# Ten f32 products per half on TensorE in the first block's attention, with a result that nobody reads

## The reference

```python
def mixer_ab(h, w_in, ...):        # layer 0
    qa, ka, va, qb, kb, vb = jnp.split(h @ w_in, AB_SPLITS, axis=-1)
    oa = causal_block_attention(qa, ka, va, map_w, bias_a)   # 4 heads, two softmax maps each
    oa = oa * lax.rsqrt(jnp.mean(jnp.square(oa), -1, keepdims=True) + LN_EPS)
    ob = dilated_attention(qb, kb, vb, table)                # 8 heads of 64
    return jnp.concatenate([oa, ob], axis=-1) @ w_o

def mixer_cd(h, w_in, ...):        # layer 1
    oc = moba_attention(qc, kc, vc, table)                   # 8 heads of 64, causal with 256 tokens
    od = causal_block_attention(qd, kd, vd, ones, fox_bias)  # 8 heads, forget bias
    return jnp.concatenate([oc, od], axis=-1) @ w_o
```

## Time and profile before

| | |
|---|---|
| median of 3 runs | 2954.01 us |
| profiled execution, its own time | 2952.88 us |
| its span, first to last instruction | 2950.4 us |
| mean granted TensorE clock | 0.932 of full |
| attention of layer 0, first score to last values | 160.8 to 222.1 us |
| attention of layer 1, first score to last values | 595.9 to 672.1 us |
| f32 products as records | two records each on TensorE; a transpose leaves one |

### The profile page before, as it was taken

The page is one execution under the profiler, slowest core; times in us unless marked ns, Lnnn a source line. Parts: engine busy times, 40 slices in busy tenths (PEclk is TensorE's granted clock), DMA queues, the critical chain, the costliest instruction groups (busy, mean ns, idle before and its releaser), DMA issues. The chain is left out here.

```text
span 2950.4 us, 39864 instructions
## 1 busy us (share of the span) xinstructions
PE 2676.7 (91%) x15451; PEld 2244.4 (76%) x15451; DVE 1807.7 (61%) x3288; ACT 1078.8 (37%) x2037; POOL 225.2 (8%) x167
## 2 busy tenths in 40 slices
PE   4757998998999799998998889999899998998899
PEld 4736997867998588886855668887688886856899
DVE  6567776537776656545748476554566544847554
ACT  2343543433443323223226343322333222326553
POOL 2000100000100201001000020000110000100110
PEclk8868998957999899999989999999999999889999
DMA  8923874802675144332720133433343433720453
GB/s 290 281 75 128 269 254 128 266 29 101 234 243 194 50 150 143 125 121 83 212 72 1 44 100 129 157 122 107 100 143 129 153 111 107 208 77 19 144 178 132
DMA packets 355605, 413.92 MB, mean 140 GB/s; under 512 B 25708, under 2 KB 292629, under 8 KB 355353
## 3 DMA queue, kind: packets, MB, share of 16 engines
q1 hardware_dynamic: 353326, 404.37, 42.6%
q0 software_dynamic: 736, 4.58, 0.5%
q10 hardware_dynamic: 1354, 2.43, 0.2%
HBM read 409.75 MB, written 5.27 MB: 141 GB/s over the span
## 5 line engine op out<-in xcount | busy, mean ns | idle before, releaser
L636 DVE TENSOR_TENSOR weight_lo<-raw_weights,weight_hi 128x512 fp32r<-128x512 f32 x1024 | 776.6, 765 | 902.9 <-ACT weight_hi L1164 892.5
L1164 ACT ACTIVATE weight_hi<-raw_weights 128x512 fp32r<-128x512 f32 x1024 | 633.0, 629 | 1336.9 <-PE bank L841 1186.4
L841 PE MATMUL bank<-H_hi,weight_hi 128*128 128x256 f32 (+1 forms) x2832 | 970.3, 343 | 116.1 <-POOL H_lo L802 82.6
L841 PE MATMUL bank<-H_lo,weight_hi 128*128 128x256 f32 (+1 forms) x2832 | 952.4, 336 | 0.0
L841 PE MATMUL bank<-H_hi,weight_lo 128*128 128x256 f32 (+1 forms) x2832 | 952.3, 336 | 0.0
L841 PEld LDWEIGHTS bank<-H_hi,weight_hi 128*128 128x128 f32 x2832 | 553.8, 196 | 193.5 <-issue 115.2
L841 PEld LDWEIGHTS bank<-H_hi,weight_lo 128*128 128x128 f32 x2832 | 554.3, 196 | 51.0
L841 PEld LDWEIGHTS bank<-H_lo,weight_hi 128*128 128x128 f32 x2832 | 555.3, 196 | 48.5 <-issue 0.5
L1451 DVE SCALAR_TENSOR_TENSOR ada_partial<-raw_weights,silu_c,ada_partial 128x512 f32<-128x512 f32 x672 | 477.8, 742 | 1.2 <-DVE ada_partial L1451 0.2
L841 PE MATMUL bank<-hidden_hi,weight_hi 128*128 128x256 f32 (+1 forms) x1056 | 361.2, 342 | 3.4 <-DVE weight_lo L636 3.4
L841 PE MATMUL bank<-hidden_hi,weight_lo 128*128 128x256 f32 (+1 forms) x1056 | 357.7, 339 | 0.0
(11 more groups left out here) (165 smaller groups left out, 2103.1 us busy)
## 6 DMA issues: line engine op xcount, KB each, us to landing
raw_weights<-in_w_ada_dram SPq DMA_DIRECT2D x120, 1024.0 KB, 5.4
raw_weights<-in_w_ffn_up_dram SPq DMA_DIRECT2D x88, 1024.0 KB, 5.3
raw_weights<-in_w_ffn_in_dram SPq DMA_DIRECT2D x44, 1024.0 KB, 5.7
raw_weights<-in_w_ffn_down_dram SPq DMA_DIRECT2D x32, 1024.0 KB, 5.1
raw_weights<-in_w_in_dram SPq DMA_DIRECT2D x18, 1024.0 KB, 7.9
raw_weights<-in_w_ffn_out_dram SPq DMA_DIRECT2D x16, 1024.0 KB, 7.7
raw_weights<-in_w_in_ab_dram SPq DMA_DIRECT2D x12, 1024.0 KB, 9.1
raw_weights<-in_w_in_cd_dram SPq DMA_DIRECT2D x12, 1024.0 KB, 7.6
```

Source lines behind the costliest of these rows:

```text
L636: eng.tensor_tensor(WL[:, p.g % SPLIT, 0:p.kt * CW].rearrange("p (t n) -> p t n", n=CW), raw_ap(ch.n, ch.kt, CW)[:, p.k0:p.k0 + p.kt, :], ...
L841: return pe.matmul(o, w, x, start=start, stop=stop, skip_group_check=True)
L1164: act.activation(WH[:, p.g % SPLIT, 0:p.kt * CW].rearrange("p (t n) -> p t n", n=CW), raw_ap(ch.n, ch.kt, CW)[:, p.k0:p.k0 + p.kt, :], ACT ...
```

## The change

`attn` gets a helper `busy(h, n)` that issues n products of `ident` with `ones`, 128x128 by 128x128 in f32, into the bank that the next `turn` overwrites. It signals nothing and nothing reads its result. It acts where a half has fewer than four key blocks and `vrow` is D, that is in layers 0 and 1, and leaves out the two halves after `sub_sums`, 12 and 13 of layer 0, whose banks hold the sums. Each round issues five before the scores and five before the turn; in rounds 14 and 15 there are no scores, and ten stand together. That is 14 + 16 halves of ten, 300 products. The new field `layer` of `state` is not read by any instruction. The lines of TensorE's functions shift by 8, so that L1077 becomes L1083.

```diff
-    state = {"q_in": 0, "normed": None, "hosted": 0}
+    state = {"q_in": 0, "normed": None, "hosted": 0, "layer": 0}
...
-        state.update(q_in=st.done, normed=None, hosted=st.hosted)
+        state.update(q_in=st.done, normed=None, hosted=st.hosted, layer=layer)
...
         def attn(s):
+            def busy(h, n):
+
+                after_sub = s.sub and h.n in (s.sub[1] + 1, s.sub[1] + 2)
+                for _ in range(n if h.nb < 4 and h.vrow == D and not after_sub else 0):
+                    mm(B_T[h.cp % 2][:, 0:P], ident[:, :], ones[:, :], True, True)
+
             def score(h):
...
             score(hs[0])
             score(hs[1])
             for i, h in enumerate(hs):
+                busy(h, 5)
                 if i + 2 < len(hs):
                     score(hs[i + 2])
+                busy(h, 5)
                 turn(h)
                 if i:
                     values(hs[i - 1], (i - 1) // 2)
```

## The result

The change makes the kernel slower by 0.9%: 2980.55 us, the median of 4 runs (2976.14 to 2986.32), against 2954.57 us, the median of 4 runs of the kernel before; the ratio is 1.0091, 95% interval 1.0068 to 1.0113. Measured once more beside other runs of the kernel before it was 2979.72 against 2951.22 us, ratio 1.0106 (1.0092 to 1.0119). The forecast was slower, 2963.5 us with a range of 2951 to 2981; the time lies just inside that range's upper end, and the step of some 26 us is two and a half times the 10.6 forecast.

The account below looks back on a forecast made before the run. It took layer 0's first halves as bound by the path scores, maxima, join, turn, and layer 1 by TensorE's 1.2 GHz clock. Layer 0 +10.7 and layer 1 -0.1 gave +10.6 on 2952.88: 2963.5 us, range 2951 to 2981.

Parts of the forecast that it names:

- The path in layer 0: Layer 0's first halves: scores, maxima, join, turn form the path; products behind scores cost nothing, those ahead 2.2 us a pair.
- turns 1 to 7: Layer 0, halves 2 to 7, three pairs: 7.73 us a pair instead of 7.45, +0.8 us.
- Start: Layer 0 up to turn 1: first products at half clock until it rises, +2.6 us, ends 1.3 and 4.5.
- Halves 8 to 11: Layer 0 up to turn 12: 40 products add 8.8 us, idle absorbs 1.0, half-clock work saves 1.6: +6.2 us.
- Tail: Layer 0, turn 13 to projection: ten products at half clock, ten at full, +3.8 us, ends 2.3 and 8.1.
- Projections: Output projections start at full clock, saving 45% of 6.1 us in layer 0 (-2.7) and of 3.3 in layer 1 (-1.5).
- Layer 1: Layer 1 with 160 products: full clock saves 32.5 us, 150 products add 33.0, idle absorbs 0.9; -0.1 us with projection.
- the early fall: Layer 1's beginning: the clock's fall at 597.96 us may not be prevented, a late rise costing 1.5 to 2.7; put at +1.0.
- The price: One full-array f32 product on TensorE, two records of 0.11 us: 0.22 us at full clock, bounds 0.214 and 0.256, 0.44 at half.
- The cheap product: Rival, 265 products on the path: 0.128 us each, sum -13.8, 2939.1 us, faster; chance 0.12.
- the hidden handovers: Rival: TensorE takes in waits of scores and turns during products, 60 groups save 9.6 us, 2953.9 us, no change; chance 0.22.
- The low clock: Rival, both attentions: clock stays at 1.2 GHz despite the products, sum +119, 3072 us; chance 0.08.

## Why the prediction was right or wrong

The forecast was right in sign and near in size in layer 0 (+11.3 with its projection, +10.7 forecast), in part by luck: the higher price of a product and the earlier rise of the clock partly cancel. It failed in layer 1. That the total still lies inside the range is luck too, since its upper end was added up from a price of 0.256, late rises and a half-clock tail, not from falls of the clock. Point by point, in the first pair of profiles:

- **The path in layer 0.** Products ahead of the scores are on it, those behind are hidden: shown by taking out the ones or the others (5.62 and 7.84 us a pair beside 7.86). Forecast for turns 1 to 7 +0.8, measured 23.56 against 22.35, +1.2.
- **Start.** Forecast +2.6 up to turn 1; measured 10.04 against 8.29, +1.75. The clock rose at 164.4 us, five microseconds after the first scores.
- **Halves 8 to 11.** Forecast +6.2, measured 18.24 against 11.48, +6.8.
- **Tail.** Forecast +3.8 from turn 13 to the projection; measured 12.07 against 7.98, +4.1, ten products at half and ten at full clock, as assumed.
- **Projections.** Forecast -2.7 and -1.5; measured -2.7 and -1.4.
- **Layer 1.** This step failed. The prediction put it as 32.5 us of half-clock work saved against 33.0 added, "-0.4", with the clock at 1.00 throughout; measured from turn 0 to the last values was 84.8 against 73.1, +11.7. Up to turn 0 it was 4.0 against 3.1 us, +0.9 as forecast (+0.8), and the early fall that was priced at +1.0 did not come: the clock held until 635.4. Two things are in the +11.7. The clock fell four times in or just behind scores and bias products, 8 us; I had named falls between halves as what would make the prediction wrong, but priced none, although the rows showed that exactly these records run at half clock for over 70 us. Full clock for all of layer 1 was the assumption that had no row behind it. And the product costs 0.25, 150 x 0.03 = 4.5 us.
- **The price.** 0.22 was taken because the new groups wait for no semaphore of their own. Inside a group that was right: the records start 0.112 us apart (169.862 and 169.974). The rest is at the ends of a group: from the last record to the scores behind it 0.205 us (170.867 to 171.072), and behind 64-column values or scores from the first record to the second 0.214 (609.492 to 609.706). So five products last 1.21 or 1.31 us, 0.25 us each. The second of these gaps lies inside a group that waits for no semaphore; what causes either, no run separates. The transposes' 0.128, which stood as the upper bound and has a handover in it, was the nearer row. On 265 products this is 8 us over both layers, of which 0.9 were given back by the earlier rise at layer 0's start.
- **The rivals.** The cheap product did not come: it needed less than 0.18 us. Nor did the hidden handovers: each new group added 0.09 to 0.19 us of its own. The low clock came in parts of layer 1 only, and wholly when the products had 8 rows (3084.92 us).
- **The reference time.** The forecast was made against one execution. Layer 1 before is 77.2 or 71.3 us by the clock's own chance, so its mean lies 2.4 us lower than the profile that I used.

## What to carry to other kernels

Work whose only purpose is to keep TensorE's clock up has to be paid at its place on the path: behind something that another engine must answer it was free here, ahead of it it cost 0.25 us apiece. Before adding any, list the longest stretches of the stage without a full-array product and put some of it into them: moving five products into such a stretch, with the number unchanged, took the falls away (89.8 to 83.3 us). Then watch the number as well: with half of them in the same places the clock fell again. And count what the filler costs against what the clock gives in each stage apart: here 50 products in one stage brought 0.2%, 300 in two cost 0.9%.

## What was not expected of the hardware

- TensorE without a gap did not raise its clock while the added records used few rows: 80 us at 1.2 GHz with 8-row products between scores and transposes.
- The clock fell from 2.4 to 1.2 GHz while TensorE was busy without a gap, in or behind 3.4 us of 64-row and 8-row products. With ten full-array products a round, five of them in the middle of that stretch, it held; with five, seven or three, some of them in the middle, it fell in places (34, 44 and 72 us at half clock).
- The same instructions ran at either clock: layer 1's bias halves without products stayed at 1.2 GHz in three executions, and in four the clock rose before any product (for some 10 us in the two that had none later).
